# Five norm borders: the last product chunk by token tiles, the next stage's first chunk by halves of 256 tokens

## The reference

```python
def rms_norm(x, g):
    y = x * lax.rsqrt(jnp.mean(x * x, axis=-1, keepdims=True) + EPS)
    return y * g

for l in range(DEPTH):                       # DEPTH = 2
    h = rms_norm(x, attn_pre_g[l])
    proj = h @ w_in[l]                       # stage in0, in1
    ...                                      # two kinds of attention -> mixed
    x = x + rms_norm(mixed @ w_out[l], attn_post_g[l])                     # stage out0, out1
    h = rms_norm(x, ffn_pre_g[l])
    y = (silu(h @ w_gate[l]) * (h @ w_up[l])) @ w_down[l]                  # ffn0/down0, ffn1/down1
    x = x + rms_norm(y, ffn_post_g[l])

# third layer
proj = rms_norm(x, norm1_g) @ w_in           # stage in2
...                                          # -> mixed (stage branch2)
h = x + mixed @ w_out                        # stage out2, no norm of the product
hn = rms_norm(h, norm2_g)
return h + (silu(hn @ w_gate) * (hn @ w_up)) @ w_down                      # ffn2, down2
```

## Time and profile before

| | |
|---|---|
| median of 3 runs | 2254.35 us (2251.06 to 2255.6) |
| the profiled execution's own time | 2254.23 us |
| its span, first to last instruction | 2252.4 us |
| TensorE matmuls busy | 2149.5 us, 95% of the span, 10268 instructions |
| VectorE, ScalarE, GpSimd busy | 768.0, 742.9, 846.3 us |
| mean granted TensorE clock | 0.983 |
| chain that ended last | PE 85%, DVE 7%, issue 5%, ACT 2%, POOL 1% |

### The profile page before, as it was taken

How to read it: one execution, slowest core, us unless ns; L and a number is a source line. 1 busy time by engine, 2 the same in 40 slices (tenths; PEclk the granted TensorE clock), 3 DMA queues, 4 the chain that set the end, 5 groups by cost and what they waited for, 6 DMA issues and landing times.

```text
span 2252.4 us, 27470 instructions
## 1 busy us (share of the span) xinstructions
PE 2149.5 (95%) x10268; PEld 1760.5 (78%) x10268; DVE 768.0 (34%) x1445; ACT 742.9 (33%) x1231; POOL 846.3 (38%) x390
## 2 busy tenths in 40 slices
PE   7999999999999999999999999999788899999999
PEld 5886778888887877778888877877677677888887
DVE  5327442121013137341212023677576332221200
ACT  4236442222223136442222233544432334222221
POOL 3430134444434420234444434433344334444443
PEclk9999999999999999999999999999999999999999
DMA  6320023332333320023332322211111223333232
GB/s 190 103 84 1 11 78 109 99 96 94 101 87 94 93 75 1 29 85 98 98 93 93 98 70 75 66 57 48 47 47 38 64 76 112 94 101 95 89 103 70
DMA packets 138736, 178.21 MB, mean 79 GB/s; under 512 B 19857, under 2 KB 87697, under 8 KB 138641
## 3 DMA queue, kind: packets, MB, share of 16 engines
q1 hardware_dynamic: 137024, 175.25, 25.8%
q10 hardware_dynamic: 1616, 1.64, 0.2%
HBM read 174.76 MB, written 2.10 MB: 79 GB/s over the span
## 4 chain that ended last, share of the span: by engine, by line
PE 85%; DVE 7%; issue 5%; ACT 2%; POOL 1%; DMA 0%; POOLq 0%; ACTq 0%; SPq 0%; DVEq 0%
PE PS L1340 24%; PE PS L1342 24%; PE PS L1341 24%; PE PS L1547 3%; PE PS L1559 2%; DVE R L1252 1%; PE PS L1714 1%; POOL w_lo L505 1%; PE PS L1535 1%; PE PS L1346 1%; PE PS L1486 1%; PE PS L1621 1%; PE PS L1650 1%; DVE R L1247 1%; DVE X L1106 0%
## 5 line engine op out<-in xcount | busy, mean ns | idle before, releaser
L505 POOL TENSOR_TENSOR w_lo<-R,w_hi 128x1024 fp32r<-128x1024 f32 (+1 forms) x268 | 629.9, 2352 | 908.4 <-ACT w_hi L580 908.3
L580 ACT ACTIVATE w_hi<-R 128x1024 fp32r<-128x1024 f32 (+1 forms) x268 | 278.3, 1041 | 949.0 <-PE PS L1342 935.8
L1340 PE MATMUL PS<-xt_hi,w_hi 128*128 128x512 f32 x1120 | 446.1, 398 | 3.4 <-DVE xt_lo L924 3.4
L1342 PE MATMUL PS<-xt_hi,w_lo 128*128 128x512 f32 x1120 | 438.3, 391 | 0.0
L1341 PE MATMUL PS<-xt_lo,w_hi 128*128 128x512 f32 x1120 | 438.1, 391 | 0.0
L1340 PE MATMUL PS<-w_hi,xt_hi 128*128 128x512 f32 x928 | 382.1, 412 | 12.2 <-DVE xt_lo L924 9.7
L1342 PE MATMUL PS<-w_hi,xt_lo 128*128 128x512 f32 x928 | 365.7, 394 | 0.0
L1341 PE MATMUL PS<-w_lo,xt_hi 128*128 128x512 f32 x928 | 365.2, 394 | 0.0
L1340 PEld LDWEIGHTS PS<-xt_hi,w_hi 128*128 128x128 f32 x1120 | 211.8, 189 | 47.7 <-issue 5.3
L1342 PEld LDWEIGHTS PS<-xt_hi,w_lo 128*128 128x128 f32 x1120 | 211.6, 189 | 44.5
L1341 PEld LDWEIGHTS PS<-xt_lo,w_hi 128*128 128x128 f32 x1120 | 211.9, 189 | 43.7 <-issue 1.0
(11 more groups left out here) (231 smaller groups left out, 2228.2 us busy)
## 6 DMA issues: line engine op xcount, KB each, us to landing
R<-in_w_in SPq DMA_DIRECT2D x48, 512.0 KB, 3.7
R<-in_w_gate SPq DMA_DIRECT2D x88, 256.0 KB, 2.8
R<-in_w_up SPq DMA_DIRECT2D x88, 256.0 KB, 3.0
raw<-in_w_in SPq DMA_DIRECT2D x44, 512.0 KB, 3.6
R<-in_w_down SPq DMA_DIRECT2D x40, 512.0 KB, 3.8
R<-in_w_ffn_gate SPq DMA_DIRECT2D x44, 256.0 KB, 2.8
R<-in_w_ffn_up SPq DMA_DIRECT2D x44, 256.0 KB, 3.1
R<-in_w_ffn_down SPq DMA_DIRECT2D x20, 512.0 KB, 3.8
```

The lines of the kernel that those rows point to most:

```text
L505: nc.gpsimd.tensor_tensor(w_lo[:, r, 0:subs, :], raw_of(stage)[:, r, 0:subs, :], w_hi[:, r, 0:subs, :].bitcast(F32), ALU.subtract).then_in ...
L580: nc.scalar.activation(w_hi[:, r, 0:subs, :], raw_of(stage)[:, r, 0:subs, :], ACT.Copy).then_inc(hi_ready, 1)
L1340: mm(out_, a_hi, b_hi, start=start, stop=False)
L1342: return mm(out_, a_lo, b_hi, start=False, stop=stop)
```

## The change

1. **Last chunk by token tiles** (`token_chunk`, tiled). All four slots of the last lap are now by tile: tile 0 whole, tile 1 whole, then tiles 2 and 3 slot by slot together. Before the last slot of tile 2 stand the first eight transposes of the next stage.
2. **First chunk of the next stage in halves** (`chunk_by_half`, `turn_half`). Tokens 0 to 255 go through all eight `k` first, then tokens 256 to 511. The weights stay in their slots for both halves, and `w_used` is counted only in the second half. In the ffn stages this makes two matmuls of 256 columns out of one of 512; in the in stages the count is unchanged. The transposes come in four groups of eight: half 0 `k` 0 to 3 (inside the product before), half 0 `k` 4 to 7 (before `k` = 2), half 1 `k` 0 to 3 (before `k` = 7 of half 0), half 1 `k` 4 to 7.
3. **Order of ScalarE and VectorE** (`norm_follows`, `half_hi`, `half_lo`): post and norm of tiles 0 and 1, then the copies of half 0, then post of tiles 2 and 3, the second copies of half 0, the norms of tiles 2 and 3, the copies of half 1.
4. **GpSimd's waits** (`lo_lap`): the low part of slot 0 of the next stage's first lap waits for the residual of tile 1, slot 1 for the normed tile 1, slot 3 for the residual of tile 3.
5. **Bank sets and memory views.** The sets of the out, ffn, down and out2 stages are exchanged so that transposes find free banks; the buffers of the gained product are laid out by `k` so that they can share memory with `xt_hi` and `xt_lo` block by block.

```diff
-SETS = {..., "out2": (1, 0)}
+SETS = {..., "out2": (0, 1)}
-        YG_down = at1(0, T, D)
+        YG_down = at1(0, KD * SEQ).rearrange("p (k t n) -> p t k n", t=T, n=P)
 ...
             def lo_lap(stage, lap, lap3):
                 for r, subs in enumerate(lap_subs(stage, lap3)):
+                    if stage in BY_HALF and isinstance(lap, int):
+                        seen = 4 * (BY_HALF[stage] - 1)
+                        if r == 0:
+                            pool.wait_ge(x_ready, seen + 2)
+                        elif r == 1:
+                            pool.wait_ge(xn_ready, T * TS_OF[stage] + 2)
+                        elif r == 3:
+                            pool.wait_ge(x_ready, seen + 4)
                     pool.wait_ge(hi_ready, 4 * lap + r + 1)
 ...
+            def norm_follows(stage, post):        # ScalarE
+                n = BY_HALF[stage]
+                post(0)
+                norm_tile(n, 0)
+                post(1)
+                hi_first(stage, [0])
+                norm_tile(n, 1)
+                hi_first(stage, [1, 2])
+                half_hi(stage, 0, range(4))
+                post(2)
+                post(3)
+                hi_first(stage, [3])
+                half_hi(stage, 0, range(4, KD))
+                norm_tile(n, 2)
+                norm_tile(n, 3)
+                half_hi(stage, 1, range(KD))
 ...
+            def norm_follows(stage, post):        # VectorE
+                n = BY_HALF[stage]
+                for t in range(2):
+                    post(t)
+                    norm_tile(n, t)
+                half_lo(stage, 0, range(4))
+                post(2)
+                post(3)
+                half_lo(stage, 0, range(4, KD))
+                norm_tile(n, 2)
+                norm_tile(n, 3)
+                half_lo(stage, 1, range(KD))
 ...
+            def chunk_by_half(stage, s):          # TensorE
+                for half in range(2):
+                    for r in range(R):
+                        if half == 0:
+                            pe.wait_ge(lo_ready, 4 * LAP0[stage] + r + 1)
+                        for sub in range(2):
+                            k = 2 * r + sub
+                            if half == 0 and k == KD - 1:
+                                turn_half(stage, 1, range(4))
+                            if k == 2:
+                                turn_half(stage, half, range(4, KD))
+                            pe.wait_ge(ts_lo, TS0[stage] + KD * half + k + 1)
+                            ...
 ...
-                for t in range(T):
-                    ...
-                    for r in range(tail[1], R):
-                        if t == 0:
-                            pe.wait_ge(lo_ready, 4 * (lap + laps - 1) + r + 1)
+                for t in range(2):
+                    for r in range(R):
+                        if t == 0:
+                            pe.wait_ge(lo_ready, 4 * (lap + laps - 1) + r + 1)
+                        last = tile_product(t, r, k0[r], k0[r] == 0)
+                    last.then_inc(tile_done, 1)
+                for r in range(R):
+                    if r == R - 1 and next_stage:
+                        turn_half(next_stage, 0, range(4))
+                    last = tile_product(2, r, k0[r], k0[r] == 0)
+                    if r == R - 1:
+                        last.then_inc(tile_done, 1)
+                    last = tile_product(3, r, k0[r], k0[r] == 0)
+                    last.then_inc(w_used, 1)
```

More of the change, by code:

```diff
@@ L104 @@
 FFN_SEEN = {"ffn0": 0, "ffn1": 11, "ffn2": 22}
-SETS = {"in": (3, 3), "out": (1, 1), "ffn": (0, 0), "down": (1, 1), "in2": (1, 1), "branch": (2, 2), "out2": (1, 0)}
+SETS = {"in": (3, 3), "out": (1, 1), "ffn": (0, 0), "down": (1, 1), "in2": (1, 1), "branch": (2, 2), "out2": (0, 1)}
 SET0 = {}
@@ L312, in build @@
         const_total = []
+        BY_HALF = {"ffn0": 1, "in1": 2, "ffn1": 3, "in2": 4, "ffn2": 5}
         TS_OF = {"in0": 0, "out0": 1, "ffn0": 2, "in1": 3, "out1": 4, "ffn1": 5, "in2": 6, "branch2": 7, "out2": 8, "ffn2": 9}
+        TS0, _n = {}, 0
+        for _stage in TS_OF:
+            TS0[_stage] = _n
+            _n += 2 * KD if _stage in BY_HALF else KD
         weights = {}
@@ L336, in first_set, with turn_bank, half_bank @@
         def first_set(stage):
-            return 1 if is_down(stage) else 0
+            return 0 if is_down(stage) else 1
+        def turn_bank(stage):
+            return 0 if stage.startswith("out") or is_ffn(stage) else 4
+        def half_bank(stage, half, k):
+            return turn_bank(stage) + (2 if half == 1 and k < 4 else 0) + k % 4 // 2
         def is_ffn(stage):
             return stage.startswith("ffn")
-        TAIL = 1
         TILED = ["out0", "down0", "out1", "down1", "out2", "down2"]
@@ L556, in _ @@
                 else:
-                    with pool.Fori(0, laps) as chunk:
+                    seen = 1 if stage in BY_HALF else 0
+                    for chunk in range(seen):
+                        lo_lap(stage, LAP0[stage] + chunk, 0)
+                    with pool.Fori(seen, laps) as chunk:
                         lo_lap(stage, LAP0[stage] + chunk, 0)
@@ L1381, in use_slot, with turn_half @@
                 return last
-            def token_chunk(stage, lap, s, laps, first, tiled=False):
+            def turn_half(stage, half, ks):
+                if ks[0] == 0:
+                    pe.wait_ge(xn_ready, T * TS_OF[stage] + 2 * half + 2)
+                else:
+                    pe.wait_ge(ts_lo, TS0[stage] + KD * half + 4)
+                for k in ks:
+                    for t in range(2):
+                        a = k % 2 * 256 + t * P
+                        last = nc.tensor.transpose(PS[:, half_bank(stage, half, k), a:a + P],
+                                                   XN[:, 2 * half + t, k * P:(k + 1) * P], ident[:, :])
+                    if k % 2:
+                        last.then_inc(ts_mm, 2)
@@ L1385, in token_chunk @@
+            def token_chunk(stage, lap, s, laps, first, next_stage=None, tiled=False):
                 a_hi, a_lo = (ht_hi, ht_lo) if is_down(stage) else (xt_hi, xt_lo)
                 kn = KF if is_down(stage) else KD
-                tail = (laps - 1, TAIL) if tiled else (laps, 0)
+                tail = (laps - 1, 0) if tiled else (laps, 0)
                 k = 0
@@ L1569, in _ @@
                 transposed_start(f"out{l}")
[L1570 to L1571 removed]
+                two_chunks(f"out{l}", f"ffn{l}")
                 swiglu(f"ffn{l}")
[L1573 to L1574 removed]
+                two_chunks(f"down{l}", f"in{l + 1}")
             for c in range(2):
                 set_free("in2", c, c)
[L1579 removed]
+                if c == 0:
+                    chunk_by_half("in2", 0)
+                else:
+                    token_chunk("in2", LAP0["in2"] + c, c, 1, False)
             def in2_products(c, r):
```

194 lines of the change are left out of this document (99 added, 95 removed).

## The result

| | before | after |
|---|---|---|
| median, same chip, 4 runs each | 2253.46 us (2251.06 to 2255.6) | 2226.92 us (2221.79 to 2228.98) |
| ratio | | 0.9879, 95% 0.9866 to 0.9891 |
| profiled execution, span | 2254.23, 2252.4 us | 2227.03, 2225.0 us |
| mean granted clock | 0.983 | 0.994 |

The change is faster by 1.2%; 2232 us was forecast, with 2222 to 2245 as range. The page after, its first part, answers to the earlier trace rows: 288 matmuls more, three stages of 96, and yet less busy time.

What follows compares the result with a forecast made beforehand. TensorE was taken as the bound, losing time at five borders through chain breaks and half clock. Stretches of 273.5 us were to become 250.6, 22.9 us less, plus 0.45 in down2: 22.4 us, so 2232 us, range 2222 to 2245.

Steps and rivals of the forecast that it cites:

- The frame: Five border stretches hold 273.46 us; the 41.9 us beyond matmul and transpose pace goes if TensorE always finds work.
- Narrow matmuls: First chunk of each ffn stage: 192 matmuls of 256 columns at 0.118 us cost 0.9 us more a stage.
- loads not hidden: Rival, 6%: each 256-column matmul in ffn pays its weight load, 0.11 us more, 63 us in all, 2295 us.
- the rule on weight loads: Trainium skill's rule: loads overlap running matmuls only when the row group differs, so each matmul here would pay its load.
- Slot 3 too late for tile 0: Last lap: tile 0 waits for slot 3's low part, 0.45 us at down0, 4.3 us in out2, none at out0.
- The norm chain: Borders: normed tiles and half 0's copies come late, 0.6 us at out0 and out1; 0.7, 0.4 and 0.75 us at down0.
- slot 0's low part starts when the residual of tile 1 is there (T + 3.7 to 4.1): Norm chain after tile 1 ends at T: normed tile at T + 7.5 to 7.9, a 0.7 us wait in down stages.
- A second reading: GpSimd's waits in `lo_lap`: by the exclusive lock rule they protect only the residual additions.
- In2: Down1 to in2 reloads in place: 3.4 us wait for normed tile 1, in all 5.0 us of waiting.
- The clock term: Half clock after in2's 3.4 us wait: 1.0 us.
- Clock at the other borders: Clock kept at 1.00 at the first three borders; 2.5 us of half clock for out2's 4.3 us wait.
- the rival in which everything is hidden: Rival, 13%: GpSimd's lock costs less than counted and no clock is lost; 30 us less, 2224 us.

Runs made afterwards that it cites:

- the run that kept the clock: Slot 3 of tiles 0 and 1 put behind their other slots in out2's last lap, against the kernel after: 2224.06 us, ratio 0.9871.
- the version with both repairs: Kernel after with slot 3 last in out2's last lap and, at in2, norm squares and half 0's copies ahead of work waiting for loads: 2223.29 us, ratio 0.9871.

## Why the prediction was right

**The frame.** The excess of 41.9 us came from paces of 0.2267 and 0.12 us. Out0 and out1 have no step over 0.5 us and are 48.5 us long, against 47.4 + 0.9 = 48.3. The frame holds to 0.25 us.

**Narrow matmuls** (0.9 us a stage, rival "loads not hidden"). Pace 0.12 us in three stages, and over 5760 matmuls in the run with all chunks narrow. The rival is out, and so is, for this kernel, the rule on weight loads that the prediction names beside it: no run shows a load being paid.

**Slot 3 too late for tile 0.** Down0 0.44 us for 0.45, out2 3.94 for 4.3. The run that moved slot 3 behind took wait and half clock away: 5.7 us.

**The norm chain.** Right in kind, off in size at both ends. At the out borders I had 0.6 us for the normed tile 3; nothing was waited. At down0 I had 0.7 us for the normed tile 1; it was 1.50. The step that failed is "slot 0's low part starts when the residual of tile 1 is there (T + 3.7 to 4.1)". VectorE, first tile 1's residual at down0, then its norm beside that low part:

```profile
661.53 0.15 DVE L1151 SCALAR_TENSOR_TENSOR small<-ssq,vbase 128x1 f32<-128x1 f32 x1
...
662.90 1.28 DVE L1161 SCALAR_TENSOR_TENSOR X<-R,small,X 128x1024 f32<-128x1024 f32 x1
...
665.94 0.75 DVE L935 TENSOR_TENSOR small<-small 128x1 f32<-128x1 f32 x1 [0.38 <-ACT small L644]
...
667.11 0.76 DVE L947 TENSOR_SCALAR R<-X,small 128x1024 f32<-128x1024 f32 x1
```

T is 666.42 - 30 x 0.2267 = 659.62 (the product's end before the turn, less 30 matmuls). The residual ends at 664.18, T + 4.56: tiles are 4.8 us apart in a down stage, not 5.4, so tile 0's norm stands in front of tile 1's residual on ScalarE and VectorE; there it starts only as L947 of tile 0 ends (660.86 + 0.75). The normed tile is there at 667.87, T + 8.25, and all of the down0 border came to 2.75 us where I had 2.3. A second reading was wrong: the waits on GpSimd protect not only the residual additions. Slot 1's protects the normed tile, which took 2.80 us without it.

**In2.** 3.51 us for 3.4 at the turn; the mechanism (high part of slot 0 ahead of the squares) is in ScalarE's timeline:

```profile
1319.13 1.06 ACT L603 ACTIVATE w_hi<-raw 128x1024 fp32r<-128x1024 f32 x1 [3.81 <-DMA raw<-in_w_in]
1320.09 1.04 ACT L640 ACTIVATE R<-X 128x1024 f32<-128x1024 f32 x1
```

Of two later waits, forecast as 0.35 and 0.8 us, the first is absent in after, where the product at half clock asks later, and the second is 0.36; in the run that kept the clock they are 0.39 and 0.42 us. The clock term was mis-sized: 1.0 us, against 6.8 us at half clock, which cost 2.1 to 2.3 (51.39 or 51.87 - 49.27, the latter less the 0.3 us longer wait).

**Clock at the other borders.** Kept at the first three, as forecast. Of the variants only two had half clock there: the one without GpSimd's waits at down0 (waits of 3.03 and 2.37 us), and the one with tiles in turn at all three (3.7 us each). For out2 I had 2.5 us; 3.4 us at half clock cost 1.6.

**Sum.** 250.6 forecast, 250.47 measured: -7.9, -6.3, -8.3, -2.5, +2.0 by border, against -7.6, -6.8, -8.0, -3.7, +3.2. The errors of 0.3 to 1.2 us cancel: that the sum fits to 0.1 us is luck, and so is much of the fit at the last two borders, where half clock varies from run to run.

**What I left out.** The median came 5 us below the forecast, about the 5 us outside the borders. That is nearer to the 2224 us of the rival in which everything is hidden, but its mechanism is not what is seen: small instructions did wait for low parts, and the clock fell at in2 and out2. These are half-clock stretches that come and go: at 42 us in one profile of the same kernel and not in the next, at in2 behind an equal wait in two kernels and not in a third. The one behind branch2 was missing in both profiles of after and in the version with both repairs, but there in six variants that don't touch this place; the 3.4 us near 1669 (1695 in before) are missing in the same three profiles and there in the same six. That speaks more for chance than for the change; the runs don't settle it. The nine timed runs of after spread over 2221.5 to 2232.6 us, with mean clocks of 0.996 and 0.990 at the two ends; the version with both repairs took 2216.95 us at 0.997 and 2224.59 at 0.992.

## What to carry to other kernels

At a border where a norm or a sum over the full width breaks the product chain, keep TensorE busy by finishing the first half of the rows early and starting the next product on them; the price is narrower matmuls, read from two starts in a row of that width. Then look at every engine's queue behind each new wait, above all for weight work that stands ahead of the chain, and at what releases it: where two tiles' products in turn released it 4.1 us later, 26 us gained became 11 lost. Moving that work behind the chain gained nothing by itself; the low parts then ran into the next residual. And an engine beside which VectorE's instructions stretch can be better idle than early.

## What the runs showed of the hardware that was not expected

- A whole-tile VectorE instruction between SBUF operands took 2.80 us beside a GpSimd subtraction, 0.75 without; one-column instructions of 0.15 us took up to 2.37.
- A wait of the same length at the same place was followed by half clock in one kernel and not in another: at in2 3.19 us and then 6.8 us at 0.50, 3.21 and then 3.4 us, or 3.20 us and none; behind branch2 3.66 us and then 10.2 us, or none. Seen lengths were 3.4, 6.8 and 10.2 us.
- Matmuls of 256 columns with a weight load each ran at 0.12 us over whole stages, those of 512 at 0.2267: narrower ones cost 6% more for the same work. This was forecast, from two rows.
